# Inputs laid out on the host, transposes of the opening left out, and the first norm applied behind the products

## The chip, the cores and the metric

The kernel runs as one program on one core of a Trainium2 chip. The metric is the device time of one execution in microseconds. The core has five engines with queues of their own: TensorE (PE in the rows, its weight loads PEld), VectorE (DVE), ScalarE (ACT), GpSimd (POOL) and SyncE (SP). SP, ACT and POOL also issue transfers; all of them run on the same 16 DMA engines, those of SP in queue q1, of ACT in q10, of POOL in q0.

## The reference, cut to what matters

A forward pass of two layers over 512 tokens of width 1024, in float32. Layer 0 mixes with a gated MLP and an S5 state space model, layer 1 with an mLSTM and block attention; both then attend to 256 memory tokens and pass a mixture of 16 experts, of which each token takes two.

```
mkv = rmsnorm(mem, mem_norm_g) @ w_mem_kv
h = x
for layer in range(2):
    xn = rmsnorm(h, norm_mix_g[layer])
    mix = even_mixer(xn, ev_w_in, ...) if layer % 2 == 0 else odd_mixer(xn, od_w_in, ...)
    h = h + mix
    h = h + cross_attn(rmsnorm(h, norm_xa_g[layer]), mem_k, mem_v, ...)
    h = h + hier_moe(rmsnorm(h, norm_ffn_g[layer]), ...)

# even_mixer: z = xn @ w_in; gelu of the first 1024 columns feeds the gated MLP, the last 512 go to S5
# hier_moe: hid = silu(t @ w1[e]) * (t @ w3[e]); y += gate[e] * hid @ w2[e], for the two experts of a token
```

## The kernel before, in words

Everything lives in SBUF tiles of 128 partitions; the order on each engine is the order of the code in its block, and semaphores join the engines. `uses_of_banks` lists, step by step, which of the eight PSUM banks a product fills; `claim`, `fill`, `await_filled`, `evac` and `taken` are the waits and signals on a bank.

- **Panels.** Each weight matrix outside the experts is read in panels of 1024 x 512 (2 MB) into one of two slots `W[0]`, `W[1]`, always by SP (`load_panel`, L559), each when the last product with the panel before it in the slot is done. A partition gets eight pieces of 2 KB.
- **Opening on TensorE.** After a warming run of products with the identity (L844) it transposes a row of gains (L878), `mem` (L883), all small vectors and the S5 rates (L891 to L893); then the products of `mem` with panel `kv0` (L903), transposes of the S5 matrices (L914), `kv1`, the 32 transposes of `h` (`transpose_gain_norm("mix_norm0")`, L838), `kv2` and `kv3`; then transposes `bT` of the S5 tables (L926), the product `s5u` with panel `ev2` in three passes of split fp32 (`split_gemm`, L865), small S5 products (`w`, L940), the transposes of the keys (`memKT`, L951) and of the gating weights (`ws`, L959), and the chunks of the S5 scan.
- **Opening on the others.** SP issues `mem`, panel 0, seven strided S5 loads (L618), panel 1 and `x` in four parts (L621), in that order; later 13 small loads (L630). ACT issues ten rows of vectors, squares `mem` and `x` row by row (L1567, L1517), takes the roots, and copies products out. VectorE evacuates the transposes, makes the S5 tables with `combine` (three steps of 128x512, L2166 to L2168), scales `h` by the reciprocal root of each token (L2173), and makes the low halves `xlo` of the transposed `h` (L2045) while ScalarE makes the high halves `xhi`.
- **Experts.** `experts(l)` handles slots of 128 token rows, one expert each, four in a quad. ScalarE writes normed rows into `xn` (L1773), with the columns regrouped by a stride of eight, and stores them to device memory `xs` (L1778). GpSimd gathers the rows of slots 1, 2, ... from there (L732); slot 0 is made by products with one-hot matrices (L1170). SP loads, for each slot, `w1` and `w3` (two loads of 1 MB, L570) and `w2` (1 MB, L573), both with 8 KB per partition. TensorE transposes the gathered rows (L1208) and runs the up products (L1219, L1230, L1235) and the down products (L1264).

Of the kernel before, what the change touches and what calls it, by code (L numbers as in the profile page):

```python
# [22 lines left out]
F32 = mybir.dt.float32  # L23
# [8 lines left out]
P = 128  # L32
# [8 lines left out]
def uses_of_banks(layers):  # L41

    steps = [("mg", 1, (7,)), ("cols", 1), ("memT", 4), ("kv0", 2), ("ct", 2), ("kv1", 2), ("mix_norm0", 8), ("kv2", 2), ("kv3", 2), ("bT", 8),
# [35 lines left out]
def program(nc, A, out):  # L79
# [7 lines left out]
    G, GI, NS = A["s5_b_re"].shape[1], A["s5_b_re"].shape[3], A["s5_b_re"].shape[2]  # L87
    LC = P // GI
    NC = T // LC
    NE, FF = A["moe_w1"].shape[1], A["moe_w1"].shape[3]  # L90
# [8 lines left out]
    with ctx:  # L99
# [35 lines left out]
        strict = E[1][:, 2048 + P:2048 + 2 * P]  # L135
# [8 lines left out]
        cols = sb("cols", [P, P])  # L144
# [5 lines left out]
        rw = sb("rw", [P, 2, KT, 20])  # L150
        rbias = sb("rbias", [P, 2, 20])
        ifw = sb("ifw", [P, KT, 8])
        ifb = sb("ifb", [P, 1])
        gbs = sb("gbs", [P, 4])
        st = sb("st", [P, 256])
        junk = sb("junk", [P, 256])
        rows = junk[:, 0:P]
        iot = E[1][:, 2048:2048 + P].bitcast(I32)
# [7 lines left out]
        fgain = sb("fgain", [P, 2, KT])  # L166
# [8 lines left out]
        names = """x_in rows_in small_in s5_in lam_in zeros_ready s5_b2 rstd_ready consts_ready mem_rstd wide_in mem_in panel0 panel1 x_hi w_hi w_lo w_used  # L175
# [66 lines left out]
        NROWS = at  # L242
# [5 lines left out]
        w_kv = A["w_mem_kv"].rearrange("(k p) n -> p k n", p=P)  # L248
        w_ev = A["ev_w_in"][0].rearrange("(k p) n -> p k n", p=P)
        w_evo = A["ev_w_out"][0].rearrange("(k p) n -> p k n", p=P)  # L250
        w_glu = A["s5_w_glu"][0].rearrange("(k p) n -> p k n", p=P)
        w_od = A["od_w_in"][0].rearrange("(k p) n -> p k n", p=P)
        w_odo = A["od_w_out"][0].rearrange("(k p) n -> p k n", p=P)
        w_q = [A["xa_wq"][l].rearrange("(k p) n -> p k n", p=P) for l in range(2)]
        w_o = [A["xa_wo"][l].rearrange("(k p) n -> p k n", p=P) for l in range(2)]
        panels, pnum, slot_of = [], {}, []

        def panel(name, src, last):
            pnum[name] = len(panels)
            slot_of.append(1 - slot_of[-1] if slot_of and name != "out10" else 0)  # L260
            panels.append((src, last))

        for n in range(4):
            panel(f"kv{n}", w_kv[:, :, n * 512:(n + 1) * 512], first[f"kv{n}"] + 1)
        for n, s in ((2, "s5u"), (1, "v0"), (0, "u0")):
            panel(f"ev{n}", w_ev[:, :, n * 512:(n + 1) * 512], first[s] + 3)
        panel("glu", w_glu, first["glu2"] + 1)
        for n in range(2):
            panel(f"out0{n}", w_evo[:, :, n * 512:(n + 1) * 512], first["out0"] + 4 * n + 3)
        for l in range(2):  # L270
            if l == 1:
                q0 = 4 * MIX + 8
                for n, (s, k, c) in enumerate((("dq", 3, q0), ("dk", 3, q0 + 512), ("qk", 3, 0), ("qk1", 3, 512),
                                               ("og", 3, 1536), ("v", 3, 1024), ("dv", 3, q0 + 1024))):
                    panel(f"od{n}", w_od[:, :, c:c + 512], first[s] + k)
                for n in range(2):
                    panel(f"out1{n}", w_odo[:, :, n * 512:(n + 1) * 512], out1_bank(n, 3))
            for n in range(2):
                panel(f"wq{l}{n}", w_q[l][:, :, n * 512:(n + 1) * 512], first[f"q{l}"] + 4 * n + 3)
            for n in range(2):  # L280
                panel(f"wo{l}{n}", w_o[l][:, :, n * 512:(n + 1) * 512], first[f"wo{l}"] + 4 * n + 3)
# [34 lines left out]
        two_parts = [first["mix_norm0"] + k for k in range(8)] + \  # L316
# [6 lines left out]
        rope_c = A["rope_cos"].rearrange("(a p) d -> p a d", p=P)  # L323
        rope_s = A["rope_sin"].rearrange("(a p) d -> p a d", p=P)
        w1 = A["moe_w1"].rearrange("l e (p k) f -> (l e) p k f", p=P)
        w3 = A["moe_w3"].rearrange("l e (p k) f -> (l e) p k f", p=P)
        w2 = A["moe_w2"].rearrange("l e (p k) d -> (l e) p k d", p=P)
# [75 lines left out]
        def row(name):  # L403
            return rows[vec[name][0]:vec[name][0] + vec[name][1], :]

        rows_loads = [(row("mem_norm_g"), A["mem_norm_g"].rearrange("(r c) -> r c", c=P))]
        for name in ("norm_mix_g", "norm_xa_g", "norm_ffn_g", "xa_qn_g", "xa_kn_g"):
            rows_loads.append((row(name), A[name].rearrange("l (r c) -> (l r) c", c=P)))
        rows_loads += [(row("ml_conv_w"), A["ml_conv_w"][0].rearrange("w (r c) -> (w r) c", c=P)),
                  (row("ml_conv_b"), A["ml_conv_b"][0].rearrange("(r c) -> r c", c=P)),  # L410
                  (row("s5_b_glu"), A["s5_b_glu"][0].rearrange("(r c) -> r c", c=P))]
        small = []
        for l in range(2):
# [2379 lines left out]
```

## Time and profile before

| | before |
|---|---|
| median of 3 runs | 1185.88 us (1180.0 to 1188.48) |
| the profiled execution | 1182.34 us |
| its span on the chip | 1180.6 us |
| TensorE busy | 1143.7 us, 97% of the span |
| VectorE, ScalarE, GpSimd busy | 701.5, 620.2, 375.9 us |
| moved by DMA | 213.21 MB |
| granted TensorE clock, mean | 0.99 |

The span is the time between the first and the last event in the profile; the execution's own time is a little longer. Busy times overlap between engines. An engine that is busy the whole time can still hold the end back, but only what stands on the chain that ended last moves the end; the rows below are of that chain, of the waits on it and of the engines and queues that it waits for.

### The profile page before, as it was taken

What the parts mean: (1) busy time and instruction counts of PE and PEld (TensorE: products, weight loads), DVE (VectorE), ACT (ScalarE), POOL (GpSimd) and SP (SyncE); (2) the same over time, 40 slices, a digit from 0 to 9 for tenths busy, and PEclk for the clock granted to TensorE, in tenths of its full rate; (3) what the DMA queues carried; (4) which work ended last, traced back from release to release, by engine and by line L of the source; (5) the groups of instructions that cost most, each with busy time, mean ns of one, the idle gap of its engine ahead of it and who ended that gap; (6) DMA issues with size and microseconds to landing.
All of it is one profiled execution on the core that took longest, in us unless ns stands there. A gap on an engine that the chain in (4) does not pass through costs nothing.

```text
span 1180.6 us, 15588 instructions
## 1 busy us (share of the span) xinstructions
PE 1143.7 (97%) x5302; PEld 859.4 (73%) x5302; DVE 701.5 (59%) x1253; ACT 620.2 (53%) x1190; POOL 375.9 (32%) x347
## 2 busy tenths in 40 slices
PE   8899999999999899999999999999999998999998
PEld 5457876788778567777778887678887785677776
DVE  4797443422332878888645893682313418888886
ACT  2734255445543467777634354444365525677773
POOL 2024350564223021111536654353442130311113
PEclk9899999999999999999999999999999999999999
DMA  9542232278200999998732221022322009899968
GB/s 295 153 143 80 32 117 72 80 288 345 72 1 16 379 367 394 395 377 297 139 120 81 72 84 60 1 72 72 131 83 72 1 1 379 340 398 382 385 263 187
DMA packets 77644, 213.21 MB, mean 181 GB/s; under 512 B 24039, under 2 KB 24979, under 8 KB 65272
## 3 DMA queue, kind: packets, MB, share of 16 engines
q1 hardware_dynamic: 64688, 180.22, 41.1%
q0 software_dynamic: 10048, 27.20, 8.0%
q10 hardware_dynamic: 2840, 4.91, 1.1%
q8 instruction: 40, 0.66, 0.2%
q14 instruction: 28, 0.23, 0.1%
HBM read 187.90 MB, written 32.51 MB: 187 GB/s over the span
## 4 chain that ended last, share of the span: by engine, by line
PE 83%; DMA 5%; DVE 5%; ACT 4%; issue 2%; SPq 1%; POOL 0%; DVEq 0%; ACTq 0%; POOLq 0%
PE bank L865 39%; PE bank L1235 8%; PE bank L1264 8%; PE bank L1230 6%; DMA xs<-E 2%; PE bank L1088 2%; PE bank L1110 2%; PE bank L903 2%; PE bank L1287 2%; PE bank L1049 1%; DMA h<-in_x 1%; SPq L618 1%; DVE E2r L2492 1%; PE bank L838 1%; ACT E2r L1818 1%
## 5 line engine op out<-in xcount | busy, mean ns | idle before, releaser
L695 POOL TENSOR_TENSOR wlo<-W,whi 128x512 fp32r<-128x512 f32 x176 | 256.2, 1468 | 423.9 <-ACT whi L1494 420.3
L1494 ACT ACTIVATE whi<-W 128x512 fp32r<-128x512 f32 x176 | 108.1, 631 | 242.8 <-PE bank L865 223.2
L865 PE MATMUL bank<-whi,xTr 128*128 128x512 f32 x480 | 192.8, 402 | 1.2 <-ACT E L1986 0.6
L865 PE MATMUL bank<-wlo,xTr 128*128 128x512 f32 x416 | 162.4, 390 | 0.0
L865 PEld LDWEIGHTS bank<-whi,xTr 128*128 128x128 f32 x480 | 90.5, 188 | 22.1 <-POOL wlo L695 2.0
L865 PE MATMUL bank<-whi,E4r 128*128 128x512 f32 x256 | 99.8, 390 | 0.0
L1235 PE MATMUL bank<-E4r,E1r 128*128 128x512 f32 x360 | 99.0, 424 | 0.0
L865 PEld LDWEIGHTS bank<-wlo,xTr 128*128 128x128 f32 x416 | 78.4, 188 | 16.6 <-issue 1.2
L2088 DVE TENSOR_TENSOR h<-bank,h 128x512 f32<-128x512 f32 x32 | 21.8, 692 | 115.0 <-PE bank L865 115.0
L1235 PEld LDWEIGHTS bank<-E4r,E1r 128*128 128x128 f32 x360 | 67.7, 188 | 27.1 <-issue 14.1
L1264 PE MATMUL bank<-whi,E2r 128*128 128x512 f32 x240 | 82.7, 405 | 2.0 <-DVE E2r L2492 0.3
L865 PE MATMUL bank<-whi,E0r 128*128 128x512 f32 x160 | 63.7, 398 | 0.0
L865 PE MATMUL bank<-whi,E2r 128*128 128x512 f32 x160 | 62.4, 390 | 0.0
L865 PE MATMUL bank<-wlo,E0r 128*128 128x512 f32 x160 | 62.3, 389 | 0.0
L729 POOL COPY st<-sm 128x1 f32 x24 | 4.4, 181 | 180.4 <-PE bank L1208 180.4
L1264 PEld LDWEIGHTS bank<-whi,E2r 128*128 128x128 f32 x240 | 45.0, 187 | 18.4 <-DVE E2r L2492 9.5
L903 PE MATMUL bank<-W,E 128*128 128x512 f32 x128 | 55.5, 593 | 1.5 <-DMA W<-in_w_mem_kv 1.5
L865 PEld LDWEIGHTS bank<-whi,E4r 128*128 128x128 f32 x256 | 48.0, 188 | 10.2
L732 POOL DMA_INDIRECT E<-xs,idx x30 | 39.7, 1322 | 25.8 <-POOL idx L730 25.8
L1264 PE MATMUL bank<-wlo,E2r 128*128 128x512 f32 x120 | 46.9, 391 | 0.0
L903 PEld LDWEIGHTS bank<-W,E 128*128 128x128 f32 x128 | 24.1, 190 | 30.8 <-issue 29.2
L1794 ACT ACTIVATE E4r<-W 128x512 fp32r<-128x512 f32 x56 | 33.3, 627 | 22.6 <-DVE sm L2457 18.1
(507 smaller groups left out, 2489.0 us busy)
## 6 DMA issues: line engine op xcount, KB each, us to landing
E<-in_moe_w SPq DMA_DIRECT2D x48, 1024.0 KB, 11.6
W<-in_moe_w SPq DMA_DIRECT2D x32, 1024.0 KB, 10.2
xT<-in_moe_w SPq DMA_DIRECT2D x16, 1024.0 KB, 15.2
W<-in_od_w_in SPq DMA_DIRECT2D x7, 2048.0 KB, 8.4
ybuf<-E SPq DMA_DIRECT2D x26, 512.0 KB, 8.0
ybuf<-memV POOLq DMA_DIRECT2D x12, 1024.0 KB, 19.9
W<-in_w_mem_kv SPq DMA_DIRECT2D x4, 2048.0 KB, 9.8
W<-in_xa_wq SPq DMA_DIRECT2D x4, 2048.0 KB, 7.9
```

The costliest lines, as they stand in the source:

```text
L695: pool.tensor_tensor(wlo[s_ % RING][:, :], slot(name)[:, block_of(name, k), :], whi[s_ % RING][:, :].bitcast(F32), ALU.subtract).then_inc( ...
L732: pool.indirect_dma_start(xg[par], None, xs[l], bass.IndirectOffsetOnAxis(ap=idx[:, par:par + 1], axis=0), bounds_check=T - 1, oob_is_err= ...
L865: ins = pe.matmul(bank(u + t)[:, :], a, b, start=(k == 0 and n == 0), stop=(k == KT - 1 and n == 2))
L903: ins = pe.matmul(bank(u)[:, :], memnT[:, k, t * P:(t + 1) * P], slot(f"kv{n}")[:, k, :], start=(k == 0), stop=(k == KT - 1))
L1088: ins = pe.matmul(bank(u)[:, head * NM:(head + 1) * NM], qT[:, k, t * P:(t + 1) * P], memKT[:, k, :], start=(kk == 0), stop=(kk == 1))
L1110: ins = pe.matmul(bank(u)[:, :], memV[:, k, n * XD + d * P:n * XD + (d + 1) * P], pT[:, n, k, :], start=(k == 0), stop=(k == 1))
L1230: pe.matmul(banks[2 + par][:, :], xgT[:, k, :], w13s[j][:, :, k, :], start=(k == 0), stop=False)
L1235: ins = pe.matmul(banks[2 + par][:, :], a, b, start=False, stop=(c == SPLIT - 1 and n == 2))
L1264: ins = pe.matmul(banks[5 + half][:, :], a, b[:, :], start=(k == 0 and n == 0), stop=(k == 1 and n == 2))
L1287: ins = pe.matmul(banks[b][:, :], late1h[:, n, t * P:(t + 1) * P], y[:, half * 512:(half + 1) * 512], start=(n == 0 and part == 0), stop=( ...
L1494: act.activation(whi[s_ % RING][:, :], slot(name)[:, block_of(name, k), :], ACT.Copy).then_inc(S["w_hi"], 1)
L1794: act.activation(up_hi[c].rearrange("p (n f) -> p n f", n=2), w13s[nj][:, :, KT - SPLIT + c, :], ACT.Copy)\
```

## The change

The host now hands over arrays in the shape in which the chip holds them (`laid_out`): `mem` and `x` also transposed (`memt`, `xt`), all vectors in one array (`vectors`), the S5 rates and matrices ready in rows (`s5_rows`, `s5_mats`), the gating weights transposed (`ws_t`), each panel as 16 KB per partition (`panels`), `w1` and `w3` side by side as 16 KB per partition and expert (`up`), `w2` as 8 KB (`down`). The rows of an expert's weights are now taken in natural order, so `xn` and the gated product are no longer regrouped. The first norm is no longer applied to `h`: `xhi` and `xlo` hold `x` times the gain, and the reciprocal root of each token is applied to the products, as a scale inside the two Gelu steps, and for `s5u` as a product with a row that TensorE broadcasts (`rb0`, ones times `diag0`).

```diff
@@ def uses_of_banks(layers):
-    steps = [("mg", 1, (7,)), ("cols", 1), ("memT", 4), ("kv0", 2), ("ct", 2), ("kv1", 2), ("mix_norm0", 8), ("kv2", 2), ("kv3", 2), ("bT", 8),
-             ("s5u", 4), ("w", 2), ("memKT", 4), ("ws", 1), ("uj0", 2), ...
+    steps = [("kv0", 2), ("kv1", 2), ("rb0", 1), ("kv2", 2), ("kv3", 2), ("bT", 8),
+             ("s5u", 4), ("w", 2), ("memKT", 4), ("uj0", 2), ...
@@ SP
                 def load_up(e, j):
-
-                    for n, w in enumerate((w1, w3)):
-                        sp.dma_start(w13s[j][:, n, :, :], w[e]).then_inc(m[f"w13_{j}"], 16)
+                    sp.dma_start(w13s[j][:, :, :].rearrange("p k n -> p (k n)"), up[e]).then_inc(m[f"w13_{j}"], 16)
...
-            sp.dma_start(memtok, A["mem"][0].rearrange("(a p) d -> p a d", p=P)).then_inc(S["mem_in"], 16)
-            load_panel(0)
-            for dst, src in s5_loads:
-                sp.dma_start(dst, src, allow_slow_non_contiguous=True).then_inc(S["s5_in"], 16)
+            sp.dma_start(memnT, A["memt"].rearrange("p (k n) -> p k n", k=KT)).then_inc(S["memt_in"], 16)
+            for lo, s_in in ((0, S["half_in"]), (KT // 2, landed[0])):
+                sp.dma_start(W[0][:, lo:lo + KT // 2, :], panels[0][0][:, lo:lo + KT // 2, :]).then_inc(s_in, 16)
             load_panel(1)
             for k in range(TT):
                 sp.dma_start(h[:, k, :], A["x"][0, k * P:(k + 1) * P, :]).then_inc(S["x_in"], 16)
...
+            sp.dma_start(xt0, A["xt"].rearrange("p (k n) -> p k n", k=KT)).then_inc(S["x_in"], 16)
+            sp.dma_start(wsT[:, :], A["ws_t"]).then_inc(S["wide_in"], 16)
@@ TensorE
             memory_gemm(1)
-            transpose_gain_norm("mix_norm0")
+            u = first["rb0"]
+            claim(pe, u)
+            pe.wait_ge(S["even_setup"], 1)
+            for t in range(TT):
+                ins = pe.matmul(bank(u)[:, t * P:(t + 1) * P], ones[:, :], diag0[:, t * P:(t + 1) * P], start=True,
+                                stop=True, skip_group_check=True)
+            fill(ins, u)
             memory_gemm(2)
@@ ACT
-            act.dma_start(*rows_loads[0]).then_inc(S["mem_in"], 16)
-            for dst, src in rows_loads[1:]:
-                act.dma_start(dst, src).then_inc(S["rows_in"], 16)
...
+            act.dma_start(sm[:, 0:P], A["s5_rows"]).then_inc(S["s5_rows_in"], 16)
+            act.dma_start(vectors[:, :], A["vectors"]).then_inc(S["vectors_in"], 16)
+            for n, o in ((0, 1024), (1, 3072)):
+                act.dma_start(E[4][:, o:o + 1024], A["s5_mats"][:, 1024 * n:1024 * n + 1024]).then_inc(S["s5_mats_in"], 16)
+            act.dma_start(memtok, A["mem"][0].rearrange("(a p) d -> p a d", p=P)).then_inc(S["mem_in"], 16)
...
+            squares("mix_norm0")
+            root("mix_norm0")
+            act.wait_ge(S["vectors_in"], 16)
+            for k in range(KT):
+                act.activation(xhi[:, k, :], xt0[:, k, :], ACT.Copy, scale=col("norm_mix_g", k)).then_inc(S["x_hi"], 1)
...
-                evac(act.activation(Gv[:, n, :], bank(u)[:, :], ACT.Gelu_apprx_tanh), u)
+                evac(act.activation(Gv[:, n, :], bank(u)[:, :], ACT.Gelu_apprx_tanh,
+                                    scale=rstd[:, NORMS["mix_norm0"], n:n + 1]), u)
...
-                        act.activation(xn[:, t, :].rearrange("p (k a) -> p k a", k=KT),
-                                       h[:, t, :].rearrange("p (a k) -> p k a", k=KT), ACT.Copy,
+                        act.activation(xn[:, t, :], h[:, t, :], ACT.Copy,
                                        scale=rstd[:, NORMS[f"ffn_norm{l}"], t:t + 1]).then_inc(S["xs_rows"], 1)
@@ VectorE
+            for k in range(KT):
+                ts(memnT[:, k, :], memnT[:, k, :], col("mem_norm_g", k), None, ALU.mult).then_inc(S["memn_ready"], 1)
...
-            dve.wait_ge(S["std_ready"], v.n["mean_ready"])
-            v(dve.reciprocal(rstd[:, n0, :], std[:, n0, :]))
+            combine(BB1, Fr, B1, Fi, B2)
+            combine(BB2, Fr, B2, Fi, B1, ALU.subtract)
+            for j in range(3):
+                combine(s5Qn[:, :, j, :], Lr[:, :, LC - 1 - j], BB1, Li[:, :, LC - 1 - j], BB2)
+            n0 = NORMS["mix_norm0"]
+            dve.wait_ge(S["stat_ready"], 2 + 4 * n0)
+            rstd_of(ssq[:, n0, :], std[:, n0, :], rstd[:, n0, :], D, "mean_ready", "std_ready")
             for t in range(TT):
-                ts(h[:, t, :], h[:, t, :], rstd[:, NORMS["mix_norm0"], t:t + 1], None, ALU.mult).then_inc(S["xn_ready"], 1)
...
+                ins = ts(diag0[:, t * P:(t + 1) * P], ident[:], rstd[:, n0, t:t + 1], None, ALU.mult)
+            ins.then_inc(S["even_setup"], 1)
...
+            for n in range(4):
+                u = first["s5u"] + n
+                await_filled(dve, u)
+                evac(tt(uT[:, n, :], bank(u)[:, :], rstd_row0, ALU.mult), u)
...
-            copies("s5u", 0, 4, lambda n: uT[:, n, :])
```

TensorE, from its first product to the tables of S5, before (`W` is a panel, `E` holds the transposed `mem`, `junk` the small rows):

```order
L844 MATMUL bank<-ident 128x128 x14
L878 MATMUL bank<-ident,junk 128x8
L883 MATMUL bank<-ident,E 128x128 x16
L891 MATMUL bank<-ident,junk 128x108
L892 MATMUL bank<-ident,junk 128x64
L893 MATMUL bank<-ident,junk 16x32
L903 MATMUL bank<-W,E 128x512 x16
L914 MATMUL bank<-ident,E 128x128 x8
L903 MATMUL bank<-W,E 128x512 x16
L838 MATMUL bank<-ident,h 128x128 x32
L903 MATMUL bank<-W,E 128x512 x32
L926 MATMUL bank<-ident,E 128x128 x32
```

The same stretch after the change (`h` holds `diag0` here):

```order
L789 MATMUL bank<-ident 128x128 x14
L834 MATMUL bank<-W,E 128x512 x32
L845 MATMUL bank<-h,ones 128x128 x4
L834 MATMUL bank<-W,E 128x512 x32
L856 MATMUL bank<-ident,E 128x128 x32
```

All transposes but those of the tables are gone, and the four products of `rb0` stand between the second and the third panel.

VectorE around the reciprocal root of `x`, before (L2171 is the root, L2173 the scaling of `h`, L2166 to L2168 the first `combine`, L2045 the low halves):

```order
L2156 TENSOR_SCALAR E<-E,nsgn 128x512
L2160 TENSOR_SCALAR E<-bank,sgn 128x512
L2160 TENSOR_SCALAR E<-bank 128x512
L2171 RECIPROCAL rstd<-std 128x4
L2173 TENSOR_SCALAR h<-h,rstd 128x1024 x4
L2166 TENSOR_TENSOR E<-sm,E 128x512
L2167 TENSOR_TENSOR E<-sm,E 128x512
L2168 TENSOR_TENSOR E<-E 128x512
L2045 SCALAR_TENSOR_TENSOR E1r<-bank,cols,xTr 128x512 x8
```

The same place after the change (L2061 to L2063 are the fifth `combine`, L1955 and L1959 the root of `x`, L2073 `diag0`, L2077 the low halves, L2081 the row of `rb0`):

```order
L2061 TENSOR_TENSOR E<-memKT,E 128x512
L2062 TENSOR_TENSOR E<-memKT,E 128x512
L2063 TENSOR_TENSOR E<-E 128x32x16
L1955 TENSOR_SCALAR ssq<-ssq 128x4
L1959 RECIPROCAL rstd<-std 128x4
L2073 TENSOR_SCALAR h<-ident,rstd 128x128 x4
L2077 SCALAR_TENSOR_TENSOR E1r<-E,vectors,xTr 128x512 x8
L2081 COPY memKT<-bank 128x512
```

The scaling of `h` stood ahead of all `combine` calls; now five of them stand ahead of `diag0`, and the root of `mem` ahead of these.

SP's queue from its start, after the change, and below it ACT's:

```order
L568 DMA E<-in_memt 128x2048
L570 DMA W<-in_panels 128x2048 x2
L514 DMA W<-in_panels 128x4096
L573 DMA h<-in_x 128x1024 x4
L574 DMA E<-in_xt 128x4096
L575 DMA wsT<-in_ws_t 128x512
L514 DMA W<-in_panels 128x4096 x5
```

```order
L1476 DMA sm<-in_s_rows 128x128
L1477 DMA vectors<-in_vectors 128x537
L1479 DMA E<-in_s_mats 128x1024 x2
L1480 DMA E<-in_mem 128x2x1024
L1483 ACT_TABLE_LOAD
L1483 ACTIVATE sm<-sm 128x32
```

The token-major `mem`, which was SP's first load, is now ACT's last.

## Rows read from the trace of the kernel before

**Rows 1.** the page, part 4: the chain that ended last, by engine

```profile
PE 83%; DMA 5%; DVE 5%; ACT 4%; issue 2%; SPq 1%; POOL 0%; DVEq 0%; ACTq 0%; POOLq 0%
```

**Rows 2.** chain of work, opening, 0 to 125 us: start us, us, what

```profile
34.82 1.28 ACT L1580
...
46.48 5.95 PE bank L838 x29
52.43 27.47 PE bank L903 x64
...
83.39 21.81 PE bank L865 x96
...
106.30 2.90 DVE E L2188 x8
```

**Rows 3.** timeline, TensorE: start, us, what, [idle before <-releaser]

```profile
44.58 0.30 PE L838 MATMUL bank<-ident,h 128*128 128x128 f32 x1 [3.62 <-DVE h L2173]
...
415.05 1.09 PE L1208 MATMUL bank<-ident,E 128*128 128x128 f32 x8 [1.97 <-DMA E<-xs,idx]
...
1008.34 1.09 PE L1208 MATMUL bank<-ident,E 128*128 128x128 f32 x8 [1.18 <-DMA E<-xs,idx]
```

**Rows 4.** windows of 1 us: length, TensorE busy (x), PEclk, DMA share, GB/s

```profile
45.00:46.00 1.00, 0.66 (x2) 0.50 1.06 412
51.00:52.00 1.00, 1.00 (x8) 0.61 0.80 41
420.00:421.00 1.00, 1.00 (x3) 0.79 1.06 434
```

**Rows 5.** chain of work, expert stages and one panel

```profile
394.13 14.99 DMA xs<-E
...
428.63 2.58 PE bank L1230 x6
...
438.81 2.57 PE bank L1230 x6
...
785.10 7.66 DMA W<-in_od_w_out
...
988.21 14.52 DMA xs<-E
```

**Rows 6.** DMA in 24-27, 403-406 (two), 407-408, 410-411: packets, MB, share

```profile
DMA packets 326, 1.21 MB, mean 403 GB/s; under 512 B 34, under 2 KB 34, under 8 KB 325
...
q1 hardware_dynamic: 119, 0.84, 66.6%
q10 hardware_dynamic: 119, 0.43, 35.0%
...
q10 hardware_dynamic: 16, 0.02, 6.5%
...
q1 hardware_dynamic: 30, 0.12, 29.8%
```

**Rows 7.** groups, ScalarE 380-420, VectorE 30-110: xcount | busy us, mean ns

```profile
L1773 ACT ACTIVATE E<-h,rstd 128x1024 f32<-128x1024 f32 x4 | 8.3, 2140 | 0.2 <-DVE rstd L2040 0.2
L1517 ACT ACTIVATE E<-h 128x1024 f32<-128x1024 f32 x4 | 4.2, 1048 | 7.5 <-DVE h L2088 7.5
...
L2166 DVE TENSOR_TENSOR E<-memKT,E 128x512 f32<-128x512 f32 x17 | 15.9, 934 | 0.7
```

**Rows 8.** timeline, VectorE: start us, us, what

```profile
38.30 0.19 DVE L2145 TENSOR_SCALAR sm<-memKT 128x32 f32<-128x32 f32 x1
...
41.44 0.48 DVE L2156 TENSOR_SCALAR E<-E,nsgn 128x512 f32<-128x512 f32 x1
...
46.34 0.68 DVE L2166 TENSOR_TENSOR E<-sm,E 128x512 f32<-128x512 f32 x1
...
48.39 5.77 DVE L2045 SCALAR_TENSOR_TENSOR E1r<-bank,cols,xTr 128x512 fp32r<-128x512 f32 x8
```

**Rows 9.** line L732, the gathers, all 30

```profile
DMA to landing us min/median/max: 4.4/8.7/12.2
```

More of the change, by code:

```diff
@@ L241, in program, with panel @@
             at += n
-        NROWS = at
+        cols = vectors[:, 0:at]
+        rw = vectors[:, at:at + 2 * KT * 20].rearrange("p (l k n) -> p l k n", l=2, k=KT)
+        at += 2 * KT * 20
+        rbias = vectors[:, at:at + 40].rearrange("p (l n) -> p l n", l=2)
+        ifw = vectors[:, at + 40:at + 40 + 8 * KT].rearrange("p (k n) -> p k n", k=KT)
+        at += 40 + 8 * KT
+        gbs, ifb = vectors[:, at:at + 4], vectors[:, at + 4:at + 5]
         def col(name, i):
             return cols[:, vec[name][0] + i:vec[name][0] + i + 1]
[L248 to L255, printed above, removed]
-        panels, pnum, slot_of = [], {}, []
-        def panel(name, src, last):
-            pnum[name] = len(panels)
+        panels, pnum, slot_of = [], {}, []
+        def panel(name, last):
+            n = len(panels)
+            src = A["glu"] if name == "glu" else A["panels"][n - ("glu" in pnum)]
+            src = src.rearrange("p (k n) -> p k n", n=512)
+            pnum[name] = n
             slot_of.append(1 - slot_of[-1] if slot_of and name != "out10" else 0)
@@ L313, in await_ring @@
                     await_filled(eng, panels[pnum[split_panels[i]]][1])
-        two_parts = [first["mix_norm0"] + k for k in range(8)] + \
+        two_parts = [("xt", k) for k in range(8)] + \
                     [first["xa_norm0"] + k for k in range(8)] + [first["o0"] + k for k in range(8)] + \
@@ L900, in memory_gemm @@
                     for k in range(KT):
[L901 to L902 removed]
+                        if n == t == 0:
+                            pe.wait_ge(S["memn_ready"], k + 1)
+                            if k == 0:
+                                pe.wait_ge(S["half_in"], 16)
+                            if k == KT // 2:
+                                await_panel(pe, "kv0")
                         ins = pe.matmul(bank(u)[:, :], memnT[:, k, t * P:(t + 1) * P], slot(f"kv{n}")[:, k, :],
@@ L954, in _ @@
                 u += 1
-            u = first["ws"]
-            claim(pe, u)
-            pe.wait_ge(S["wide_in"], 16)
-            for n in range(H):
-                ins = pe.transpose(bank(u)[:, n * P:(n + 1) * P], wsN[:, n, :], ident[:])
-            fill(ins, u)
             def chunk_rows(n):
```

328 lines of the change are left out of this document (126 added, 202 removed), and 2 rows, old and new, of the table steps.

## The prediction

> **What bounds the kernel now.** I read the page first, then the chain that ended last, then the opening and the two expert stages in windows. The chain is 83% TensorE [rows 1], so a change pays only where TensorE waits, where it does work that goes away, or where its clock is low. The reader is to see three such places. First the opening: until 46.5 us the chain does not run over TensorE; it goes through SP, which issues small strided loads, the landing of `x`, its squares, the S5 tables and the row scaling of `h`, and then over 32 transposes of `h` [rows 2]. TensorE is free at 40.96 us and idles 3.62 us [rows 3]; the granted clock is then 0.50 (the 1.2 GHz level) until about 51.6 us [rows 4]. Second, each expert stage: the normed rows go to device memory (`xs`) and come back by a gather, and the chain waits 14.99 and 14.52 us for the last store of `xs` to land [rows 5]; TensorE waits 1.97 us for the gather behind it in layer 0 and 1.18 us in layer 1 [rows 3]. Third, one panel of `od_w_out` is waited for 7.66 us [rows 5]. The expert turns repeat every 10.18 us (428.63 to 438.81), nearly all of it TensorE [rows 5].
>
> **The opening, step by step.** Removed from TensorE: the transposes of `mem`, of small rows, of the S5 matrices, of `h`, and the four of the gating weights. Added: four 128x128 products with ones (`rb0`). The products `kv0` to `kv3` stay, 27.47 us for two of the four panels [rows 2].
> - Start of `kv0`: it needs the host-transposed `mem` (1.05 MB), the vectors, the gain (eight VectorE steps of 128x256, the first is enough to begin; 2.90 for eight [rows 2]) and half of panel 0. The traffic runs at 1.21 MB in 3 us [rows 6], 0.40 per us. With some 2.6 MB ahead on both queues, data from 2.6 us on (an estimate) and 1.4 us from the last packet to the landing (the store of `xs` has its last 16 packets before 408 and lands at 409.12 [rows 5, 6]) that is 10.4 us. TensorE is then free for `rb0` at 10.4 + 27.4 = 37.8.
> - `rb0` waits for `diag0`, and that is a new wait: all behind it on TensorE, `kv2` first, is late with it. VectorE builds `diag0` at the end of a chain in its own order: the squares of token-major `mem`, their root, 13 small steps, five `combine` calls, the root of `x`. From the landing of `mem`: two squares of 1.05 [rows 7], a table load of 1.28 [rows 2], root and reciprocal 0.5; the small steps 3.1 (38.30 to 41.44) and five combines of 2.05 (46.34 to 48.39) [rows 8], 10.3; second root and four diagonals 1.7. Together 19.0 us behind `mem`.
> - When `mem` lands is not shown, since it moves to the end of ACT's queue. Two queues that both have work send equal numbers of packets: 119 and 119 in 3 us, 0.84 MB against 0.43 [rows 6]. ACT's queue holds 768 runs up to the end of `mem` (four loads of 128, one of 256). Beside them SP sends its first 768: 6.3 MB if a 16 KB run is one packet. With ACT's 2.4 MB that is 8.7 MB, 21.5 us, so `mem` lands at 25. Were the ACT queue not held back, it would be 17 (2.4 MB beside as many of SP's); served last, 31. I take 24.5, near the row. Then `diag0` is ready at 43.5, TensorE waits 5.7 us, `rb0` takes 0.9, and `kv2` starts at 44.4.
> - Clock. The wait of 3.62 us was followed by 6.6 us at 0.50; one of 1.97 by 3.6, until 420.6 [rows 3, 4]. So the first 6 us of `kv2` run at half speed: 3.0 us lost. `kv3` ends at 44.4 + 27.5 + 3.0 = 74.9 against 79.90 [rows 2]: **-5.0**.
> - The root of `x` does not come into it while the chain from `mem` is later: `x` and its transposed copy are through after 11.9 MB, landed at about 33.5; four squares 4.2, root and diagonals 1.8: 39.5. That is the floor for `rb0`.
> - `bT` and `s5u`. After 43.5 VectorE has eight splits (5.77 [rows 8]) and five combines (10.3) left before the first tables, done near 60; `bT` comes at 74.9: hidden. The second half (sine arguments, four steps of 2048 columns, 8 to 10 by those of 512; nine combines 18.5; some 8 us of slow steps, as the mean of 934 ns against 0.68 shows [rows 7, 8]) ends at 95 to 97. `s5u` ends at 74.9 + 3.5 + 21.8 = 100.2 [rows 2]: hidden with 3 us to spare; beyond these it would be paid one for one.
> - Behind `s5u` the norm of the keys starts later: VectorE scales the four `s5u` banks first, and ScalarE loads a table (1.28) before the root, because sine ran in between. Now the scaling ends 4.0 us behind `s5u` (109.2 against 105.2 [rows 2]); after: 0.75 + 0.2 + 0.9 + 0.5 + 2.9 = 5.3. The four transposes of the gating weights go: 0.8 at the half clock (5.95 for 29 [rows 2]), 0.5 at the full one; I take 0.6. **+0.7**.
>
> The scale inside the two Gelu steps and the product in place of the copy to `uT` replace instructions one for one beside products: nothing; uncovered, 0.07 us each (0.75 against 0.68, by the splits' 5.77 for 8 [rows 8]), 0.3 in all.
>
> **The expert stages.** ScalarE's copy into `xn` reads `h` with a stride and takes 2.14 us for 128x1024; the contiguous square of that size takes 1.05 [rows 7]. Contiguous, the first `xs` store is issued 1.05 us earlier and the last 4.3. But the stores share the engines with weights. Beside 8 KB weight packets `xs` gets a third of the bytes (0.43 of 1.27 MB [rows 6]); beside 16 KB runs of `up` it would get a fifth. It can't be later than the whole traffic: in layer 0 the weights are through between 410 and 411 [rows 6], 2 us behind `xs`. So per layer the bounds are 1.05 earlier (a 16 KB run counts as two packets) and 2.0 later (as one). Later also means a longer idle: layer 0 waits 1.97 us now and has the half clock behind it already, layer 1 waits 1.18 [rows 3] and would lose another 1.7. Ends for both layers: **-2.1 and +5.7**. No row shows a 16 KB run; I take **+1.8**, the middle.
>
> The Trainium skill says (DMA: Bandwidth & Descriptors, "Queues, rings and completion order") that an engine takes turns between queues by whole packets, each of several descriptors. The trace agrees as far as equal counts go. If it held for a whole load, `xs` would stand at the late end and the sum below 3.9 higher. It speaks against larger runs beside a short store.
>
> **Panels.** They become one contiguous run per partition. Large packets move 1.27 MB in 3 us, smaller ones 1.21 [rows 6], 5% of about 5 us: **-0.3** for the one panel that is waited for. The others land beside products. The gated product written contiguously in a turn, and two up loads made one, change nothing that the chain waits for: the turn is TensorE's.
>
> **Sum.** The profiled execution took 1182.34 us (span 1180.6): -5.0 + 0.7 + 1.8 - 0.3 = -2.8 gives 1179.5. The median of the runs shown, 1185.88, is 3.5 above that execution, and they scatter from 1180.0 to 1188.5; I predict 1180.
>
> **Rivals.**
> - *`mem` lands early, at 20 or before*: ACT's queue is served beside a cold SP queue without being held back. Then `rb0` waits only for the root of `x`: 39.5, `kv2` starts at 40.4, hardly any clock is lost, `kv3` ends at 68: -12 + 0.7. With the expert stages between -2 and +2: 1169 to 1173, say **1170**. For it: ACT's five loads are issued early, when SP has little under way. Against: the equal counts [rows 6].
> - *`mem` lands last, at 31.* `diag0` at 50, `kv3` at 81.4: +1.5 + 0.7, and `xs` at its late end: **1190**. The new wait eats what the transposes gave.
> - *A gather inside the expert turns comes late*: slower. Its two buffers alternate, so it has nearly two turns, 18 us; it lands in 8.7 us, at most 12.2 [rows 9]. Next to 16 KB runs its share falls from a third to a fifth. From 18 us on TensorE waits in every turn: one microsecond in 24 turns gives **1204**. Against: the median would have to double.
> - *Nothing changes*, because the opening is off the bound: excluded as far as the chain shows; 1182 lies inside the first case.
>
> **Chances.** My forecast 0.56; early `mem` 0.30; late `mem` 0.08; late gathers 0.06. Within 1% of 1185.88 (1174.0 to 1197.7, about what a measurement can tell from no change) lie the first and the third, so faster 0.30, same 0.64, slower 0.06. The range reaches from the early case to the late one, 1167 to 1190; the forecast's own range is 1175 to 1187.
>
> **What would show it.** `kv0` starting near 10.4; TensorE idle before `rb0`, and the granted clock behind it (0.50 for some 6 us, or no drop in the early case); VectorE waiting for the squares of `mem` until about 27; copies into `xn` of about 1.05 us; the landing of `xs` against 409.12 and 1002.73, and equal counts of packets with 16 KB runs; waits for the gather in the turns. The prediction is wrong if `mem` lands well before 22 or after 28, if `xs` lands more than 3 us from where it does now, or if a turn is not 10.18 us.

## The result, and the profile after

The changed kernel takes 1191.36 us (median of 20 executions, 1184.03 to 1193.78), the kernel before 1182.11 in the same comparison; the ratio is 1.0061, 95% interval 1.0039 to 1.0083. So it is slower by 0.6%, where 1180 and a range of 1167 to 1190 were forecast. The profiled execution took 1192.91 us (span 1191.0, mean granted clock 0.982); the one of before 1182.34 (1180.6, 0.99). Its twenty times lie in two groups, 1184.0 to 1187.7 (nine) and 1191.3 to 1193.8 (eleven), and the profile is from the upper one; what separates them is read below.

The chain that ended last, by engine (page, part 4), answers to [rows 1]: DMA has gone from 5 to 7%.

```profile
PE 84%; DMA 7%; DVE 4%; ACT 3%; issue 1%; ACTq 0%; DVEq 0%; POOL 0%; POOLq 0%
```

The opening on that chain (start us, us, what), to be read against [rows 2]:

```profile
3.01 21.98 DMA E<-in_mem
...
43.13 0.88 DVE h L2073 x4
44.06 2.07 PE bank L845 x8
46.13 29.19 PE bank L834 x64
75.32 3.74 PE bank L856 x32
79.06 21.98 PE bank L810 x96
```

`mem` lands at 24.99, `diag0` (L2073) ends at 44.01, and `kv3` ends at 75.32 where it ended at 79.90. TensorE's timeline (in brackets the idle time before and who ended it) shows the new wait, the two behind `s5u`, the products V of the S5 scan (L915), and the wait for the first gather in both layers, [rows 3]:

```profile
10.03 27.97 PE L834 MATMUL bank<-W,E 128*128 128x512 f32 x64 [3.36 <-DVE E L2017]
44.06 2.07 PE L845 MATMUL bank<-h,ones 128*128 128x128 f32 x8 [6.06 <-DVE h L2073]
...
105.81 1.97 PE L881 MATMUL bank<-ident,E 128*128 128x128 f32 x16 [2.91 <-DVE E L2101]
...
110.83 0.68 PE L900 MATMUL bank<-ident,E 64*128 64x64 f32 x8 [1.30 <-DVE E L2115]
...
115.84 12.21 PE L915 MATMUL bank<-E 128*128 128x64 f32 x64
...
419.87 1.97 PE L1131 MATMUL bank<-ident,E 128*128 128x128 f32 x8 [5.59 <-DMA E<-xs,idx]
...
1016.00 1.97 PE L1131 MATMUL bank<-ident,E 128*128 128x128 f32 x8 [4.37 <-DMA E<-xs,idx]
```

The transposes of the keys (L951, behind the wait for VectorE's scaled keys) and the same products V before the change, from the timeline of before:

```profile
109.25 3.19 PE L951 MATMUL bank<-ident,E 128*128 128x128 f32 x16 [2.19 <-DVE E L2188]
...
120.38 7.36 PE L992 MATMUL bank<-E 128*128 128x64 f32 x64
```

V started 4.5 us earlier than before and took 4.85 longer. Windows of the changed kernel show the clock over it (length, busy time and count of PE, PEld, DVE, ACT and POOL, then PEclk, DMA share, GB/s):

```profile
119.00:121.00 2.00, 2.00 (x11) 2.00 (x11) 0.00 (x0) 0.00 (x0) 0.00 (x0) 0.50 0.78 107
129.00:130.00 1.00, 1.00 (x4) 0.80 (x3) 0.00 (x0) 0.00 (x0) 0.00 (x0) 0.50 0.00 0
421.00:423.00 2.00, 2.00 (x6) 1.15 (x6) 1.81 (x3) 0.40 (x1) 0.18 (x1) 0.50 0.75 227
```

and of the kernel before, where the drop comes earlier, behind the wait for the keys; its last line is the stretch behind the panel:

```profile
108.00:112.00 4.00, 2.75 (x15) 2.76 (x16) 4.00 (x10) 3.90 (x8) 0.00 (x0) 0.73 1.05 402
...
120.00:122.00 2.00, 2.00 (x23) 1.93 (x21) 0.00 (x0) 0.60 (x1) 0.00 (x0) 1.00 0.69 86
...
796.00:798.00 2.00, 2.00 (x11) 2.00 (x11) 0.58 (x4) 2.00 (x8) 0.77 (x1) 0.50 0.03 8
```

In the changed kernel the granted clock is 0.50 from 118 until past 130 (the 1.2 GHz level), although TensorE is busy the whole time; before the change, V ran at 1.00. Behind the wait for the keys it is the other way round: the 16 transposes there took 3.19 us before and 1.97 after (L881), although the wait had grown from 2.19 to 2.91 us. At 421 the clock is low behind the wait for the gather.

The expert stages and the panel on the chain, against [rows 5]:

```profile
391.98 22.02 DMA xs<-E
...
433.78 2.58 PE bank L1153 x6
...
443.96 2.58 PE bank L1153 x6
...
790.26 8.09 DMA W<-in_panels
...
988.22 22.13 DMA xs<-E
...
1030.52 2.57 PE bank L1153 x6
```

`xs` is issued earlier by the cheaper copies (mean 1136 ns, below, against 2140 [rows 7]) and yet lands later: 22 us instead of 15 after its last issue. A turn still takes 10.18 us (433.78 to 443.96). The queues between 400 and 406 us, against [rows 6]:

```profile
q1 hardware_dynamic: 169, 1.98, 77.4%
q10 hardware_dynamic: 170, 0.63, 25.7%
```

```profile
L1694 ACT ACTIVATE E<-h,rstd 128x1024 f32<-128x1024 f32 x4 | 4.3, 1136 | 0.2 <-DVE rstd L1959 0.2
```

SP's and ACT's queues again move the same number of packets, 169 and 170, but SP's are now up to 16 KB, so `xs` gets 0.63 of 2.61 MB, 24%, where it got a third.

Where the time went, as the shift of after against before at one point each:

| point | before | after | shift |
|---|---|---|---|
| end of `kv3` | 79.90 | 75.32 | -4.6 |
| end of `s5u` | 105.20 | 101.04 | -4.2 |
| first chunk columns (L977, L900) | 115.37 | 110.83 | -4.5 |
| first swap, behind V and the first part of `v0` | 133.13 | 135.04 | +1.9 |
| turn of slot 2, layer 0 | 428.63 | 433.78 | +5.2 |
| behind the panel of `od_w_out` | 819.68 | 823.70 | +4.0 |
| turn of slot 2, layer 1 | 1020.45 | 1030.52 | +10.1 |
| span | 1180.6 | 1191.0 | +10.4 |

The opening gives its 4 to 5 us; V takes 6.4 back; the expert stages cost 3.3 and 6.1. The -1.2 in the middle is clock too. TensorE works through most of the 7.66 and 8.09 us in which the chain waits for the panel; behind them it idles for ScalarE, 2.25 us before and 2.67 after, and the ten transposes that follow took 2.35 us at 0.50 before and 1.37 at 1.00 after:

```profile
795.85 2.35 PE L1417 MATMUL bank<-ident,E 128*128 128x128 f32 x10 [2.25 <-ACT E L1956]
```

```profile
801.44 1.37 PE L1340 MATMUL bank<-ident,E 128*128 128x128 f32 x10 [2.67 <-ACT E L1875]
```

### The profile page after: what moved, and what is told of

Read it like the earlier page. It is cut to its first block, busy times and chain, and to the rows that moved or that the text cites. A ratio compares the mean times of both kernels' runs of the same rounds, so it can differ in the third digit from the quotient of the medians.

```text
span 1191.0 us, 15402 instructions
## 1 busy us (share of the span) xinstructions
PE 1145.3 (96%) x5246; PEld 857.5 (72%) x5246; DVE 697.7 (59%) x1253; ACT 611.8 (51%) x1186; POOL 371.9 (31%) x342
## 4 chain that ended last, share of the span: by engine, by line
PE 84%; DMA 7%; DVE 4%; ACT 3%; issue 1%; ACTq 0%; DVEq 0%; POOL 0%; POOLq 0%
PE bank L810 40%; PE bank L1158 9%; PE bank L1187 8%; PE bank L1153 7%; DMA xs<-E 4%; PE bank L834 2%; PE bank L1011 2%; PE bank L1033 2%; DMA E<-in_mem 2%; PE bank L1210 2%; PE bank L972 1%; DVE E2r L2398 1%; PE bank L915 1%; ACT E2r L1738 1%; PE bank L1316 1%
## 5 line engine op out<-in xcount | busy, mean ns | idle before, releaser
L810 PEld LDWEIGHTS bank<-whi,E4r 128*128 128x128 f32 x256 | 48.0, 188 | 10.1
L2254 DVE TENSOR_TENSOR E<-bank,vectors 128x512 f32<-128x512 f32 x64 | 41.4, 683 | 14.5 <-PE bank L1131 12.3
L677 POOL DMA_INDIRECT E<-xs,idx x30 | 36.6, 1221 | 26.3 <-POOL idx L675 25.1
```

Source lines behind the costliest of these rows:

```text
L677: pool.indirect_dma_start(xg[par], None, xs[l], bass.IndirectOffsetOnAxis(ap=idx[:, par:par + 1], axis=0), bounds_check=T - 1, oob_is_err= ...
L810: ins = pe.matmul(bank(u + t)[:, :], a, b, start=(k == 0 and n == 0), stop=(k == KT - 1 and n == 2))
L2254: tt(xgT[:, 4 * b:4 * b + 4, :], banks[b][:, :].rearrange("p (k t) -> p k t", k=4), last(cols[:, vec["norm_ffn_g"][0] + 8 * l + 4 * b:vec[ ...
```

## The experiments

The leading theory was two mechanisms: long runs on SP's queue starve `xs` by equal counts of packets, and the gaps behind `s5u` bring the clock down over V. The rivals: the traffic as a whole sets the landing; the drop has another cause; the new wait of `rb0` is the real loss.

**1. `up` in runs of 8 KB.**

```diff
-                    sp.dma_start(w13s[j][:, :, :].rearrange("p k n -> p (k n)"), up[e]).then_inc(m[f"w13_{j}"], 16)
+                    w, c = w13s[j][:, :, :].rearrange("p k n -> p (k n)"), 4096 // 2
+                    for i in range(2):
+                        sp.dma_start(w[:, c * i:c * i + c], up[e][:, c * i:c * i + c]).then_inc(m[f"w13_{j}"], 16)
...
```

(The waits for `w13` count 32 instead of 16.)

> The changed kernel with `up` read in two loads of 8 KB per partition instead of one of 16 KB; nothing else differs. Theory of equal counts (each of two busy queues sends as many runs as the other, whatever their size): `xs` gets a third of the bytes again instead of a quarter to a fifth, so its last store lands 15 to 17 us after its issue instead of 22.0 (layer 0) and 22.1 (layer 1), TensorE waits under 2 us for the first gather instead of 5.59, the half clock behind it shrinks, and the time falls by 8 to 14 us, to about 1179. Rival, the traffic as a whole sets the landing (it starts and ends when it did, and `xs` is among the last): `xs` lands within 1.5 us of where it does now and the time stays at 1189 to 1192.

Measured: median 1178.59, ratio to before 0.9947 (0.9920 to 0.9974). From its chain, its timeline and its queues (396 to 402 us):

```profile
392.04 17.33 DMA xs<-E
```

```profile
415.06 1.09 PE L1133 MATMUL bank<-ident,E 128*128 128x128 f32 x8 [0.74 <-DMA E<-xs,idx]
```

```profile
q1 hardware_dynamic: 237, 1.74, 68.5%
q10 hardware_dynamic: 234, 0.83, 33.8%
```

The issue stands at the same place (391.98 and 392.04), the landing 4.6 us earlier; the wait falls from 5.59 to 0.74 us and in layer 1 there is none. This undoes one part of the change, and the kernel is faster than before by half a per cent. Equal counts hold, 237 to 234, and the share is back at a third. The rival of the whole traffic falls.

**2. The gaps behind `s5u` filled.**

```diff
+            claim(pe, u)
+            fill_wait(bank_of[u], ident[:], 22)
             pe.wait_ge(S["even_setup"], 2)
...
                 u = first[f"uc{n}"]
-                taken_all(pe, f"uj{n}", 2)
                 claim(pe, u)
+                if n == 0:
+                    fill_wait(bank_of[u], ident[:], 9)
+                taken_all(pe, f"uj{n}", 2)
```

> The changed kernel with 22 idle products of 128x128 put into the 2.91 us in which TensorE waits for the scaled keys, and 9 into the 1.30 us in which it waits for the chunk copies, behind `s5u`. Theory: these gaps bring the granted clock down to 0.50 over the V products (12.14 us instead of 7.36) and the first products of `v0`. Filled, V takes 7.4 us, the product `v0` starts about 5 us earlier, and all executions lie where the faster ones of the changed kernel lie, 1184 to 1187. Rival: the drop comes from something else (the run of products before, the part of the program); then V stays at 12 us in the profile or the times stay spread from 1184 to 1194, and the median at 1191.

Measured: median 1195.24, ratio 1.0083 (1.0055 to 1.0110). TensorE's timeline:

```profile
102.48 5.18 PE L789 MATMUL bank<-ident 128*128 128x128 f32 x44
107.50 1.91 PE L883 MATMUL bank<-ident,E 128*128 128x128 f32 x16
...
118.29 11.79 PE L919 MATMUL bank<-E 128*128 128x64 f32 x64
```

The idle products took longer than the gap (5.18 against 2.91 us), so V starts 2.4 us later, and it is as slow as ever. My theory of the gaps falls: with no wait above 0.5 us for 16 us ahead of it, the clock still came down over V. The times still lie in two groups, five at 1187.8 to 1189.3 and six at 1195.2 to 1198.2.

**3. The weights held until `xs` has landed.**

```diff
-                for j in range(2):
-                    load_up(NE * l + j, j)
-                    load_down(NE * l + j, j)
+                load_up(NE * l, 0)
+                sp.wait_ge(S["xs_stored"], 16 * TT * (l + 1))
+                load_up(NE * l + 1, 1)
+                load_down(NE * l, 0)
+                load_down(NE * l + 1, 1)
                 load_up(NE * l + 2, 2)
```

> The changed kernel with SP holding all weight loads of an expert stage but the first `up` until the normed rows `xs` have landed (`up` of slot 1 and the rest are issued behind a wait for the four stores). Theory of shared traffic: `xs` has only 2 MB beside it and lands 5 to 8 us after its last issue instead of 22; the gather is in by 405 and the first transposes follow the one-hot and up products without a wait (5.59 us now) and at the full clock; the weights are through near 416, before their use; 6 to 8 us per layer, 1176 to 1179. Rival: something other than `xs` holds the first gather (the slot indices on GpSimd, or the weights of slot 1, now later): TensorE still waits 3 to 6 us, on another releaser, and the time falls by less than 4.

Measured: median 1173.44, ratio 0.9934 (0.9909 to 0.9959). The line that issues `xs` (all eight issues), the chain, and the timeline:

```profile
DMA to landing us min/median/max: 2.7/3.1/3.4
```

```profile
396.28 9.75 DMA E<-xs,idx
```

```profile
406.07 1.09 PE L1133 MATMUL bank<-ident,E 128*128 128x128 f32 x8 [0.75 <-DMA E<-xs,idx]
```

`xs` lands in at most 3.4 us, sooner than expected, the time is below the forecast 1176 to 1179, and the held weights come in time. The first gather now shares the engines with the held weights and takes 9.75 us, but TensorE waits only 0.75 for it. This execution has V at 7.35 us, with the very code of the changed kernel in the opening, and its span is 1168.4; the profile of experiment 1, again with that code, has it at 12.14. So the same code shows both. What differs ahead of V is the place of the drop: here the clock fell behind the wait for the keys, as long as in the changed kernel, and the transposes took 2.68 us instead of 1.97:

```profile
104.54 2.68 PE L883 MATMUL bank<-ident,E 128*128 128x128 f32 x16 [2.91 <-DVE E L2103]
...
114.89 7.35 PE L917 MATMUL bank<-E 128*128 128x64 f32 x64
```

**4. `rb0` behind the fourth panel.**

```diff
-            u = first["rb0"]
-            claim(pe, u)
...
             memory_gemm(2)
             memory_gemm(3)
+            u = first["rb0"]
+            claim(pe, u)
...
             copies("kv3", 0, 2, lambda n: memV[:, n, 512:1024], scale=mem_rstd)
+            copies("rb0", 0, 1, lambda n: rstd_row0)
```

> The changed kernel with the four `rb0` products behind the fourth panel of the memory instead of behind the second (ScalarE copies their bank out). Theory: the new wait of 6.06 us and the 3 us lost to the half clock behind it go, `kv3` ends near 65.5 instead of 75.3 and `s5u` near 91.5 instead of 100.9, but then TensorE waits for the second half of the tables, which VectorE ends at 95 to 96; so 4 us at most come through to the keys, and a longer idle there. Time 1186 to 1190. Rival, TensorE alone sets the opening: the whole 9.8 us come through, 1181. Second rival, the half clock merely moves to the S5 products: no gain, 1191.

Measured: median 1187.20, ratio 1.0038 (1.0014 to 1.0062), inside the 1186 to 1190. TensorE's timeline:

```profile
38.98 27.73 PE L834 MATMUL bank<-W,E 128*128 128x512 f32 x64 [1.38 <-DMA W<-in_panels]
...
73.83 2.82 PE L856 MATMUL bank<-ident,E 128*128 128x128 f32 x12 [4.04 <-ACT memV L1471]
98.39 1.94 PE L870 MATMUL bank<-E 128*16 128x128 f32 x64
```

The wait of 6.06 us goes, and 1.38 for the third panel and 4.04 for ScalarE (whose copy of `kv3` stands behind the sines, and these wait for VectorE's sine arguments, ready at 69.36) come in its place; `s5u` ends and the small S5 products begin at 98.39, 2.6 us earlier than in the changed kernel. So the number came out, but by another wait than the forecast one: VectorE's last table was ready at 95.99, and TensorE did not wait for it. Much of what the new wait cost was not there to win, because the sine arguments stood right behind it.

**5. V in four pieces between the steps of `v0`.**

```diff
-            for n in range(4):
+            def chunk_states(n):
...
-            split_gemm(first["v0"], "ev1", by_k(xhi), by_k(xlo["ev"]), between={1: [(swapped, n) for n in range(4)]})
+            split_gemm(first["v0"], "ev1", by_k(xhi), by_k(xlo["ev"]),
+                       between={0: [(chunk_states, 0)], 1: [(chunk_states, 1)], 2: [(chunk_states, 2), (chunk_states, 3)],
+                                3: [(swapped, n) for n in range(4)]})
```

> The changed kernel with the 64 narrow products V no longer in one piece ahead of the product `v0` but between its steps (a quarter behind step 0, a quarter behind step 1, half behind step 2, the swaps behind step 3). Theory: the granted clock of 0.50 from 118 to 131 us comes with V standing in one piece, whatever the gaps ahead of it, since filling these gaps left it at 11.8 us; between wide products the clock stays at 1.00 there, `v0` and V together end 6 us earlier than in the slower executions, and all executions lie at 1183 to 1187. Rival: the drop stays in about half of the executions, and the median at 1189 to 1192. Second rival: the scan, which starts some 8 us later, is then waited for at the swaps back: a few us slower than the faster executions of the changed kernel.

Measured: median 1190.70 (1190.16 to 1191.74 in six executions), ratio 1.0077 (1.0061 to 1.0093). From the timeline:

```profile
117.86 1.89 PE L915 MATMUL bank<-E 128*128 128x64 f32 x16
...
153.34 5.21 PE L929 MATMUL bank<-h,perm 128*128 128x512 f32 x8 [2.83 <-DVE h L2132]
```

The second rival comes out, and the forecast 1183 to 1187 is missed: TensorE waits 2.83 us for the scan at the swaps back, and these take 5.21 us instead of 3.67. There is no half clock over V and no scatter, as the theory said. But in this profile too the clock had fallen behind the wait for the keys (their transposes took 3.08 us), as in experiment 3, where V in one piece was not hit either; so the profile alone does not show that the pieces keep the clock up.

**6. `up` in runs of 4 KB** (the edit of experiment 1 with four loads).

> The changed kernel with `up` read in four loads of 4 KB per partition, as long as a row of `xs`. Theory of equal counts: beside `up`, `xs` now gets half of the bytes, so its last store lands 11 to 13 us after its issue in layer 0 (17.3 with 8 KB, 22.0 with 16 KB); the first gather is not waited for. The time is that of the 8 KB kernel or a little less, 1176 to 1179, since at 17.3 us only 0.74 us of waiting was left. Rival: the share does not depend on the length below 8 KB; 16.5 to 18 us again.

Measured: median 1173.71, ratio 0.9941 (0.9918 to 0.9963). Its queues from 388 to 394 us, and `xs` of layer 1 on its chain:

```profile
q10 hardware_dynamic: 339, 1.26, 51.2%
q1 hardware_dynamic: 340, 1.25, 50.9%
```

```profile
973.46 13.77 DMA xs<-E
```

339 packets against 340, and now half of the bytes. With `up` in runs of 16, 8 and 4 KB the last store of `xs` lands 22, 17.3 and at most 13.8 us after its issue. The median is 5 us below that of experiment 1 and 2 under the forecast, but no wait explains that (0.74 us for the gather in layer 0 there, 1.45 in layer 1 here): the twelve times of either kernel lie in two groups, near 1172 and near 1179, five of them in the lower one there and eight here.

**7. The norm of the keys taken earlier.** VectorE's step and ScalarE's root moved ahead:

```diff
-            for k in range(LC + 1):
-                combine(s5PP[:, :, k, :], Lr[:, :, k], C1, Li[:, :, k], C2)
+            for i in range(LC + 1):
+                if i == 4:
+                    dve.wait_ge(S["hd_sq"], 8)
+                    rstd_of(xmx[:, 0:8], xnm[:, 0:8], xrec[:, 0:8], XD, "hmean_ready", "hstd_ready")
...
+                combine(s5PP[:, :, i, :], Lr[:, :, i], C1, Li[:, :, i], C2)
```

> The changed kernel with the norm of the keys (root on ScalarE, eight scalings on VectorE) taken in the middle of the second half of the tables instead of behind `s5u`. Theory: the 2.91 us in which TensorE waits for the scaled keys go, but the chunk copies behind them wait on VectorE for ScalarE's eight copies of the `w` bank, which start only 1.5 us earlier (no table load and root ahead of them); so 1.5 us come through, 1188 to 1191. Rival: all 2.9 us come through and the clock stays up, since the gap that brings it down is gone: 1182 to 1186. Second rival: VectorE's tables end 2 us later and TensorE waits for them behind `s5u`: no gain.

Measured: median 1198.99 (1187.73 to 1201.43), ratio 1.0117 (1.0075 to 1.0159). TensorE's timeline:

```profile
103.97 3.62 PE L870 MATMUL bank<-E 128*16 128x128 f32 x64 [3.90 <-DVEq L2098]
...
119.79 13.91 PE L915 MATMUL bank<-E 128*128 128x64 f32 x64
```

The second rival, and slower than any forecast: the wait for the keys becomes a wait of 3.90 us for the tables, and the clock is low both there (3.62 for what took 1.94) and over V. VectorE has no room: in the changed kernel it works without a pause from 44 to 96 us, and here it also waits 2.03 us for ScalarE's root.

**8. The hold of experiment 3 in the kernel before** (the same edit; `load_up` there issues two loads).

> The kernel before with the one edit of the third experiment: SP holds all weight loads of an expert stage but the first `w1` and `w3` until `xs` has landed. It takes the waits for `xs` out of the old kernel too, so what is left between it and the third experiment (1173.4) is the rest of the change, above all the opening. Theory: `xs` lands 3 to 4 us after its last issue; the waits of 1.97 and 1.18 us and the half clock in layer 0 (1.7 us) go: 1177 to 1179; the opening and the panels of the changed kernel are then worth 4 to 5 us, less what the half clock over V takes. Rival: 1172 to 1174, the rest of the change is worth nothing and the third experiment's gain is the hold alone. Second rival: the copy into `xn` with a stride ends so late that TensorE waits for the gather all the same: 1181.

Measured: median 1180.41, ratio 0.9997 (0.9974 to 1.0021), which misses the 1177 to 1179. The waits for the gather do go in both layers, and the turns of layer 0 stand 5 us earlier, but at the end of that stage its chain now runs through a store of results and not through TensorE:

```profile
546.62 11.69 DMA ybuf<-E
```

So 4 us of the gain are lost there; why this store took 11.69 us I did not follow. The comparison with experiment 3 is less clean than I wanted: 1180.41 against 1173.44, 7 us, holds the opening and this tail. What it does show is that the hold alone does not explain experiment 3.

**9. Experiments 3 and 4 together.**

> The changed kernel with the hold of the third experiment and `rb0` behind the fourth panel as in the fourth. If the two gains add up (2.5 us where the fourth reached the keys earlier), 1170 to 1172. Rival: the longer or earlier idle behind `s5u` costs as much clock as it gives: 1173 to 1175.

Measured: median 1172.34 (1168.44 to 1180.23), ratio 0.9926 (0.9903 to 0.9949): 1 us under experiment 3, less than the sum, just above the 1170 to 1172, and within the scatter of the two.

**10. As 9, with V in two pieces.**

```diff
+                       between={0: [(chunk_states, 0), (chunk_states, 1)], 1: [(chunk_states, 2), (chunk_states, 3)],
+                                2: [(swapped, n) for n in range(4)]})
```

> As the ninth, with V in two pieces of 32 products behind steps 0 and 1 of `v0` and the swaps behind step 2, so that the scan starts some 2.7 us later, which is the slack seen in the fifth experiment (the swaps back came 2.7 us behind the scan in the third). Theory: no half clock over V in any execution and no wait for the scan: 1167 to 1170, all executions within 5 us. Rival: pieces of 3.7 us still bring the clock down in some executions, or the scan is waited for by some us: 1171 to 1175.

Measured: median 1169.24 (1168.75 to 1172.12 in six executions), ratio 0.9892 (0.9870 to 0.9915): 1.1% faster than before and, by the ratios to it, 1.7% faster than the changed kernel, the best of the series. Timeline, and the window of the first piece:

```profile
116.41 3.68 PE L917 MATMUL bank<-E 128*128 128x64 f32 x32
...
149.13 3.70 PE L931 MATMUL bank<-h,perm 128*128 128x512 f32 x8
```

```profile
116.00:120.00 4.00, 4.00 (x36) 3.92 (x35) 0.00 (x0) 0.00 (x0) 0.00 (x0) 1.00 0.75 101
```

Two pieces of 3.68 us each at full clock, no wait at the swaps back. Here too the clock had fallen behind the wait for the keys (transposes of 2.60 us), as in the profile of experiment 9 (2.50), where V in one piece took 7.36. What speaks for the pieces is the scatter: experiment 9 differs only here and had three of its ten executions at 1176 to 1180, with a mean granted clock of 0.984 to 0.988; none of these six lies there, and their clocks are 0.992 to 0.997. Six against ten executions leave room for chance.

## Why the prediction was wrong, step by step

**Right: the opening.** `kv0` began at 10.03 (10.4 forecast), `mem` landed at 24.99 (24.5), `diag0` was ready at 44.01 (43.5), the new wait was 6.06 (5.7), `kv3` ended at 75.32 (74.9): -4.6 for -5.0. Two sizes inside it were off and cancel nearly, which is luck: `rb0` took 2.07 instead of 0.9, since I counted its products at full speed (where they took 1.05, experiment 4), and the low clock cost `kv2` 1.7 instead of 3.0.

**Wrong: the term of the expert stages**, taken at +1.8 between -2.1 and +5.7. It measured +3.3 and +6.1, 9.4. The mechanism was in the text, the size was not. I had seen equal counts of packets and then took the middle between a 16 KB run as one packet and as two, because no row showed one; and yet for the landing of `mem` the same prediction had counted it as one. The rows of the changed kernel show one packet: 169 carry 1.98 MB, 11.7 KB each on average, more than pieces of 8 KB could, beside 170 of `xs`; and experiments 1 and 6 show the equal counts at two more lengths. The late bound itself was too low: 2.0 us per layer by the end of the traffic, where the landings came 3.0 (414.0 against 409.12 and a shift of 1.9) and 3.6 later (1010.35 against 1002.72 and 4.0), since `xs` and the weights now ended together, at the very end of the traffic. And what hangs on the landing was mis-sized: the waits grew from 1.97 to 5.59 and from 1.18 to 4.37, and in layer 1 the clock then ran low over the transposes and the next products, 1.97 and 4.93 us instead of 1.04 and 2.84 (the latter in experiment 1, without the wait), 3.0 us where I had put 1.7. The Trainium skill (DMA: Bandwidth & Descriptors, "Queues, rings and completion order") says that an engine drains a whole packet from one queue before it turns to the next. The runs agree as far as equal counts go (169 to 170 with runs of up to 16 KB); how many runs an engine drains at a turn, none of them shows. I had named that page as speaking against larger runs and did not let the sum follow it.

**Missing: V.** "Behind `s5u`" I put +0.7, and it measured -0.4 (the shift goes from -4.16 at the end of `s5u` to -4.54 at the first chunk columns): the wait for the keys grew from 2.19 to 2.91 us, but in this execution no half clock followed it. I had priced the granted clock only right behind waits. The sum had no term for a stretch where TensorE is busy and the clock falls, and that cost 6.4 us in this execution: more than the whole gain of the opening.

The profiles bear out that V separates the two groups of times: V took 12.2 us in the changed kernel, 12.1 in experiment 1, 11.8 in 2 and 13.9 in 7, whose profiled executions lie in the upper group of their kernel, and 7.4 in 3, 4, 6 and 9, which lie in the lower. They also show that the drop comes at one of two places. In eight of the twelve profiles (before, 3, 4, 5, 6, 8, 9, 10) the clock falls right behind the wait for the keys: the 16 transposes there take 2.50 to 3.19 us instead of 1.97, and V is then at full speed. In the changed kernel and in experiments 1 and 2 it does not fall there, and falls over V; experiment 7 has both. The early place is cheap: the slower transposes use up what is otherwise a wait of 1.30 us for the chunk copies, and from the first of them to the first chunk columns it takes 5.31 us in experiment 3 against 5.02 in the changed kernel.

What I can say of the cause is bounded: filling the gaps does not prevent the drop over V (experiment 2), and the same opening shows either form (experiments 1 and 3). That V in pieces between wide products is spared is likely but not shown: none of the twelve executions of experiments 5 and 10 stands apart as a slow one, but their two profiles have the early drop. Why the clock falls at one place or the other, and why the kernel before is seldom so slow (4 of 34 of its executions beside experiments 1 to 4 above 1186), is open.

**Small: the panel**, -0.3 forecast, +0.4 measured (8.09 against 7.66): with contiguous 16 KB runs this panel landed no sooner.

**The rivals.** Late gathers in the turns did not come: pitch 10.18, as forecast. Late `mem` at 1190 was near in time, but `mem` was not late; a right number there would have had a wrong reason.

**What the change is worth.** Its opening is a gain of 4 to 5 us; its 16 KB runs turn that into a loss. With the weights held, or in shorter runs, the changed kernel beats the old one (experiments 1, 3, 6).

## What to carry to other kernels

Before making the loads of one queue longer, look for a short transfer on another queue that the chain waits for: beside a busy queue it gets one packet for each of theirs, so its share falls as their runs grow; cut the runs, or hold them until it has landed. When a wait is removed, ask what stands behind it on every engine (here VectorE's sine arguments), and compare the granted clock over the busy stretches too, not only behind idle ones. Where a kernel's times lie in two groups, one profile shows one of them: find out which before a difference is put down to an edit.

## What the runs showed of the hardware that was not expected

- The clock fell to 0.50 in the middle of a busy stretch: from 118 to past 130 us with TensorE 2.00 of 2.00 us busy, the largest wait of the 6 us ahead being 0.41 us. The Trainium skill (TensorE: Matmul & The Clock Gate, "HAM oscillation — how this bites in real kernels") puts drops of the clock down to waits of TensorE between groups of products. Here filling the waits did not prevent the drop (11.79 us for V in experiment 2), and the measurement decides.
- The length of a wait does not say whether the clock falls behind it. The wait of 2.91 us for the keys was followed by the low clock in experiments 3 to 6 and by the full one in the changed kernel and experiment 1. Behind the panel, waits of 2.25 (before), 2.83 (9) and 2.92 us (6) were followed by the low clock, waits of 2.67 (after), 2.80 (3) and 3.15 us (5) by the full one.
- Two busy queues share by packets almost exactly: 169 to 170, 237 to 234, 340 to 339, where a packet of SP's queue carried 11.7, 7.3 and 3.7 KB on average (MB over packets) and one of ACT's 3.5 to 3.7.
